# Rotary halves exchanged by SBUF transfers instead of TensorE, with the sums one block later and weight chunks asked for later from another queue

## The chip, the cores and the metric

The kernel runs on one core of a Trainium2 chip. A core has five engines, each with an instruction queue of its own that runs strictly in order: TensorE (PE) for matmuls, VectorE (DVE), ScalarE (ACT), GpSimd (POOL) and SyncE (SP), which here only issues transfers (DMA). They wait for each other through semaphores. The metric is the device time of one execution, in microseconds (us). Lower is better.

## The reference

The reference runs two transformer blocks on a sequence of 256 tokens with 1024 features, in float32. What matters here is the first attention of the second block, a differential attention with 8 heads, each with two query and two key parts of 64 features. Queries and keys are rotated before they meet:

```python
def apply_rope(x, cos, sin):
    half = x.shape[-1] // 2
    x1, x2 = x[..., :half], x[..., half:]
    ...
    return jnp.concatenate([x1 * c - x2 * s, x2 * c + x1 * s], axis=-1)

def diff_attention(hn, w_qkv, w_o, lq1, lk1, lq2, lk2, subln_g, lambda_init, cos, sin):
    ...
    q = apply_rope(q.reshape(B, S, 2 * H, d), cos, sin).reshape(B, S, H, 2, d)
    k = apply_rope(k.reshape(B, S, 2 * H, d), cos, sin).reshape(B, S, H, 2, d)
    ...
        p = jax.nn.softmax(s, axis=-1)
        a = p[:, :, 0] - lam * p[:, :, 1]
        return jnp.einsum('bqhk,bkhe->bqhe', a, v)
    ...
    o = rms_norm(o, subln_g, SUBLN_EPS) * (1.0 - lambda_init)
    return o.reshape(B, S, DIFF_V_WIDTH) @ w_o
```

After it come the output projection, a squared-ReLU MLP, and a latent attention with an MLP of its own, which the change touches only through constants.

## The kernel before

All weights arrive as one stream of chunks of 1 MB, each of two units (128 partitions by 1024 floats). Five chunks fit in the buffer `raw` (`NR`). Each unit is split into a high part (`whi`, made by ACT) and a low part (`wlo`, made by DVE), which together hold the float32 value; five units fit there (`NS`). A product is three matmuls: high by high, high by low, low by high. A unit can be split once the unit five places back has been used.

`schedule()` writes one list of steps. Every engine's program walks through this same list and runs its part of each step, so the order of the list is the order on each queue. In the stage around the change, `for hh in range(8)` with g = 0 and g = 8 makes the query block and then the key block of each head: `block` is 24 matmuls in two halves of 12 with a call in between. After it stands `rope`: ACT copies the block out of PSUM into `sg`, and POOL multiplies that copy with the cosines into `hm`. Half a block later stands `rope_end`: PE multiplies the copy with the constant matrix `rot`, which exchanges the halves and puts the sign on, into the other half of the same PSUM bank; DVE multiplies that with the sines (line 2545) and adds the cosine part (two adds of 64 partitions for a query, line 2550; one for a key, line 2552). After the block, `feed()` appends a `split` of the unit that has found room, and after each second one a `load` of a chunk, which SP issues once DVE's low part of the freed units is done.

The work of the attention heads is laid between blocks by `side.nudge()`, which is called twice per block (once between its halves, once behind it) and advances at most two parts. Head `hh` starts when the rotations of its query and key were emitted at least `rest[0]` nudges ago. Its steps are `diff_masks` and `diff` (PE: 2 + 8 matmuls), `softmax` (DVE: four maxima, line 2514; ACT: four exponentials, line 2221), `diff_mix` (DVE: a reciprocal at line 2572 up to two large operations at line 2581). Four nudges later comes `p_turn` (PE transposes, line 1939) and `p_copy` (ACT), then `times_v` (PE), `diff_square` (ACT, line 2262), `rstd` (DVE line 2310, POOL line 2619), `diff_scaled` (DVE line 2280), and `diff_turn` (PE, line 1978) with the copies of `part` (ACT and DVE). Heads 6 and 7 start during the output projection that follows, in which each unit is four groups of three matmuls of 512 columns (`row` steps).

Seen from DVE, each head has a round: four maxima, a wait for ACT's exponentials, the mix, a low part, the sums of a key, the part of the head two before, `rstd` of the head before and a wait for POOL, `diff_scaled`, another low part, the sums of a query, and the next head's maxima.

The lines that say this best:

```python
    def rope_end(at, rope):
        t_q[at], born[at] = next(rope), side.now
        yield
    ...
            tk = block(b, 0, unit(("qk", g + hh)), n1, side.nudge)
            rope = roped(("kT", hh) if g else ("qT", hh), not g, b, tk, 1.0 if g else 0.125, by_r)
            next(rope)
            side.nudge()
            feed()
            side.soon(rope_end(g + hh, rope))
```

## Time and profile before

| what | value |
|---|---|
| median of 3 runs | 1132.99 us (1132.96 to 1134.18) |
| the profiled execution's own time | 1132.69 us |
| its span, first to last instruction | 1131.4 us |
| PE busy | 1118.9 us, 99% of the span |
| DVE busy | 822.2 us, 73% |
| ACT busy | 638.4 us, 56% |
| POOL busy | 54.0 us, 5% |
| granted clock of PE | 1.000 over the whole span |
| stage of the 16 blocks | from about 574.4 to 643.6 us of the span |

The busy share of an engine is an average over stages, and PE's matmul ends are modelled, so 99% says that PE seldom stood empty and not how much room other engines have. The views used below give the start of an instruction and its duration. Where an engine stood idle before an instruction, the row has in brackets for how long and what released it. Instructions of one engine overlap a little in their records, so the distance between two starts, and not the recorded duration, is what an instruction costs its queue.

### The profile page before, as it was taken

Reading aid. Unit: us, or ns where it says so; the run is one execution under the profiler, and the core shown is the slowest. Engines: PE = TensorE matmul, PEld = TensorE weight load, DVE = VectorE, ACT = ScalarE, POOL = GpSimd, SP = SyncE. Lnnn points to the kernel's source line nnn. Section 1 sums busy time; section 2 is a strip of 40 time slices with the busy share of each in tenths; the row PEclk is TensorE's granted clock in tenths of the full one; section 3 lists DMA queues with packets and bytes.
Section 4 is the critical chain, followed back from the end, with each engine's and each line's share of the span. In section 5 each row is a group of like instructions: output and inputs, shape, how many; then the busy total and the mean of one; then the engine's idle time right before and its main releaser. Section 6 shows DMA issues by size and latency. Waiting matters only on the chain.

```text
span 1131.4 us, 16859 instructions
## 1 busy us (share of the span) xinstructions
PE 1118.9 (99%) x6545; PEld 980.3 (87%) x6545; DVE 822.2 (73%) x1417; ACT 638.4 (56%) x1205; POOL 54.0 (5%) x68
## 2 busy tenths in 40 slices
PE   9999999999999999999999999999999999999997
PEld 7998989799987888888899988888889988888886
DVE  6988878798666766666777777666667866766665
ACT  6664444856757754555755556444556654555553
POOL 2100000000001000000012300000001100000000
PEclk9999999999999999999999999999999999999999
DMA  9989989494232766666453326555554434655530
GB/s 385 421 318 390 368 319 352 138 336 162 94 113 75 250 209 224 214 224 207 145 187 112 118 107 224 190 185 189 189 181 168 164 112 152 209 191 190 191 129 37
DMA packets 33920, 231.10 MB, mean 204 GB/s; under 512 B 3729, under 2 KB 5169, under 8 KB 6450
## 3 DMA queue, kind: packets, MB, share of 16 engines
q1 hardware_dynamic: 31536, 225.59, 55.1%
q10 hardware_dynamic: 2306, 4.45, 1.2%
q8 instruction: 52, 0.85, 0.3%
q14 instruction: 26, 0.21, 0.0%
HBM read 228.95 MB, written 1.07 MB: 203 GB/s over the span
## 4 chain that ended last, share of the span: by engine, by line
PE 87%; DVE 6%; ACT 4%; issue 1%; DMA 1%; POOL 1%; ACTq 0%; DVEq 0%; POOLq 0%
PE ps L1727 43%; PE pacc L1727 43%; DVE wlo L2283 1%; ACT whi L2009 1%; ACT arena L2116 1%; DMA cl<-in_cols 1%; ACT wk L2221 1%; POOL st L2619 1%; DVE st L2514 0%; PE ps L1864 0%; DVE wk L2508 0%; DVE wlo L2293 0%; PE ps L1939 0%; DVE h L2405 0%; ACT arena L2009 0%
## 5 line engine op out<-in xcount | busy, mean ns | idle before, releaser
L2283 DVE TENSOR_TENSOR wlo<-raw,whi 128x1024 fp32r<-128x1024 f32 x346 | 415.0, 1223 | 115.3 <-ACT whi L2009 114.9
L1727 PE MATMUL ps<-both,whi 128*128 128x256 f32 (+2 forms) x1728 | 457.2, 339 | 1.2 <-DVE both L2380 0.6
L2009 ACT ACTIVATE whi<-raw 128x1024 fp32r<-128x1024 f32 x346 | 360.5, 1057 | 94.8 <-PE ps L1727 49.8
L1727 PE MATMUL ps<-both,wlo 128*128 128x256 f32 x1264 | 348.6, 281 | 0.0
L1727 PEld LDWEIGHTS ps<-both,whi 128*128 128x128 f32 (+1 forms) x1728 | 294.5, 189 | 41.8 <-issue 2.7
L1727 PEld LDWEIGHTS ps<-both,wlo 128*128 128x128 f32 x1264 | 236.2, 189 | 2.9
L1727 PE MATMUL pacc<-whi,both 128*128 128x512 f32 (+2 forms) x352 | 106.4, 383 | 1.0 <-ACT both L2132 0.6
L2009 ACT ACTIVATE sg<-ps 128x256 f32<-128x256 f32 (+1 forms) x98 | 37.3, 380 | 100.3 <-PE ps L1727 100.3
L1727 PE MATMUL pacc<-whi,mhi 128*128 128x512 f32 x228 | 90.7, 398 | 0.0
L1727 PE MATMUL pacc<-whi,mlo 128*128 128x512 f32 x228 | 89.5, 392 | 0.0
L2303 DVE SCALAR_TENSOR_TENSOR raw<-raw,silu_c 128x1024 f32<-128x1024 f32 x72 | 89.4, 1249 | 0.1
L1727 PE MATMUL pacc<-wlo,mhi 128*128 128x512 f32 x228 | 89.1, 391 | 0.0
L1727 PEld LDWEIGHTS pacc<-whi,both 128*128 128x128 f32 x352 | 64.0, 188 | 13.8 <-issue 1.3
L1727 PE MATMUL pacc<-both,whi 128*128 128x256 f32 x384 | 71.8, 293 | 0.1
L1727 PE MATMUL pacc<-whi,hhi 128*128 128x512 f32 x172 | 68.1, 396 | 0.0
L1727 PE MATMUL pacc<-whi,hlo 128*128 128x512 f32 x172 | 67.4, 392 | 0.0
L1727 PE MATMUL pacc<-wlo,hhi 128*128 128x512 f32 x172 | 67.2, 391 | 0.0
L2619 POOL TENSOR_TENSOR st<-st,mod 128x1 f32<-128x1 f32 (+1 forms) x34 | 20.3, 599 | 962.1 <-DVE st L2315 795.0
L1727 PE MATMUL pacc<-wlo,both 128*128 128x512 f32 (+2 forms) x176 | 62.9, 376 | 0.0
L1727 PEld LDWEIGHTS pacc<-both,whi 128*128 128x128 f32 x384 | 58.2, 190 | 1.1 <-issue 0.2
L2352 DVE TENSOR_TENSOR hm<-ps,sg 128x256 f32<-128x256 f32 x64 | 27.1, 423 | 44.1 <-ACT sg L2009 44.0
L1727 PEld LDWEIGHTS pacc<-whi,mlo 128*128 128x128 f32 x228 | 42.8, 188 | 10.3
(283 smaller groups left out, 1473.0 us busy)
## 6 DMA issues: line engine op xcount, KB each, us to landing
raw<-in_stream SPq DMA_DIRECT2D x213, 1024.0 KB, 5.0
gates<-gate_rows ACTq DMA_DIRECT2D x3, 512.0 KB, 5.6
h<-in_x SPq DMA_DIRECT2D x2, 512.0 KB, 4.2
cst<-in_const ACTq DMA_DIRECT2D x1, 1024.0 KB, 4.8
arena<-bias_rows ACTq DMA_DIRECT2D x1, 1024.0 KB, 22.5
arena<-in_final_g SPq DMA_DIRECT2D x1, 512.0 KB, 5.7
out<-tmp SPq DMA_DIRECT2D x2, 256.0 KB, 2.0
out<-tmp ACTq DMA_DIRECT2D x2, 256.0 KB, 2.3
```

Of the source, the lines that this page charges most:

```text
L1727: return e.matmul(o, a, b, start=start, stop=stop)
L2009: return e.activation(o, a, ACT.Copy, **how)
L2116: e.activation(m.arena[:, 6144 + 512 * st.n:6656 + 512 * st.n], m.h[:, st.i, half(st.f)], ACT.Square, scale=D ** -0.5, accum_out=m.stat(st ...
L2221: e.activation(m.wk[:, st.dst, a:a + n], src[:, a:a + n], ACT.Exp, bias=m.stat(st.mx + i), accum_out=m.stat(st.sm + i)).then_inc(S["exp"], 1)
L2283: return e.tensor_tensor(o, a, hi.bitcast(F32), ALU.subtract)
L2303: e.scalar_tensor_tensor(src, src, 1.0, m.silu_c[:, :], ALU.mult, ALU.mult, accum_out=m.adac[:, k:k + 1]).then_inc(S["ada"], 1)
L2352: e.tensor_tensor(u, m.bank(st.b)[:, 0:T], m.sg[:, st.m, :], ALU.add).then_inc(S["sums"], 1)
L2619: e.tensor_tensor(m.stat(r, width), m.stat(v, width), ex, ALU.pow).then_inc(S["xr"], 1)
```

## The change

For 15 of the 16 rotations (all but the last key), the step `rope_end` is replaced. `rope_swap`: ACT copies the block from PSUM into a place in the arena (three places in turn); POOL multiplies with the cosines as before; SP waits for the copy and issues four transfers from SBUF to SBUF, each of 32 partitions by 1 KB, that put each 32 partitions where their partner half lies. `rope_close`: DVE waits for the transfers, multiplies with the sines, and adds the cosine part. The sign now sits in the sine table, and the matrix `rot` is an unsigned exchange, also for the rotations that still use it. `rope_close` stands behind the next block's `rope_swap`, ahead of the heads' steps of that place, half a block later than `rope_end` did; `rest[0]` is 3 instead of 2 in this stage, counted from there. The PSUM bank is given back when the copy is done.

In this stage the weight chunks are issued by ACT's queue instead of SP's, and their step is written one and a half blocks later: `feed()` notes it as owed, the middle of the next block makes it due, and the middle of the one after issues it. What is left at the end of the stage is issued there by two calls, still on ACT. Then loads go back to SP.

```diff
@@ -242,13 +242,27 @@
             return [(P * k, P, COLS["kv_in_g"] + k) for k in range(8)]
         return []
 
+    owed, due, loader = [], [0], ["sp"]
+
     def load_chunk():
+        if loader[0] == "act":
+            owed.append(0)
+        else:
+            load_next()
+
+    def load_due():
+        for _ in range(due[0]):
+            load_next()
+        due[0] = len(owed)
+        owed.clear()
+
+    def load_next():
         n = pos["chunk"]
         if 2 * n >= len(stream):
             return
         pos["chunk"] += 1
         free = [t for u in (2 * (n - NR), 2 * (n - NR) + 1) for t in raw_free.get(u, [])]
-        add("load", chunk=n, free=latest(*free))
+        add("load", chunk=n, free=latest(*free), lane=loader[0])
 
     def feed(until=None, limit=100):
         while not hold and limit and pos["unit"] < (until or len(stream)):
@@ -1280,6 +1294,22 @@
         ys.give(yb, t)
         yield t
 
+    slots, swaps = Places([Place(n) for n in range(3)]), Counter()
+
+    def swapped(dst, split, b, tk, s, by):
+        slot = slots.take()
+        n, (at, t_tables) = slot.at, by
+        x, y = tick("rpc"), tick("rpz")
+        swaps[n] += 64
+        add("rope_swap", b=b.at, full=tk, s=s, n=n, free=slot.free, at=at, tables=t_tables, copied=x)
+        banks.give(b, x)
+        yield
+        sine = tick("rps")
+        add("rope_close", n=n, cosine=y, swapped=(f"swap{n}", swaps[n]), sine=sine, at=at, dst=dst, split=split)
+        t = tick("rpd", 2 if split else 1)
+        slots.give(slot, t)
+        yield t
+
     turns, by_r = [], []
 
     def during_v():
@@ -1353,17 +1383,34 @@
         t_q[at], born[at] = next(rope), side.now
         yield
 
+    pending, rest[0], loader[0] = [], 3, "act"
+
+    def halfway():
+        load_due()
+        side.nudge()
+
     for hh in range(8):
         for g in (0, 8):
             if hh == 7:
                 banks.retire(fix[2:4] if g else fix[0:2])
             b = banks.take()
-            tk = block(b, 0, unit(("qk", g + hh)), n1, side.nudge)
-            rope = roped(("kT", hh) if g else ("qT", hh), not g, b, tk, 1.0 if g else 0.125, by_r)
+            tk = block(b, 0, unit(("qk", g + hh)), n1, halfway)
+            last = g and hh == 7
+            rope = (roped if last else swapped)(("kT", hh) if g else ("qT", hh), not g, b, tk, 1.0 if g else 0.125, by_r)
             next(rope)
+            if pending:
+                at, was = pending.pop()
+                t_q[at], born[at] = next(was), side.now
             side.nudge()
             feed()
-            side.soon(rope_end(g + hh, rope))
+            if last:
+                side.soon(rope_end(g + hh, rope))
+            else:
+                pending.append((g + hh, rope))
+    load_due()
+    load_due()
+    loader[0] = "sp"
+    rest[0] = 2
     while banks.leaving:
         side.step(False)
     cross = Whole([(n1, ("cl", COLS["mlp_g"]), None, list)])
@@ -1548,7 +1595,7 @@
 
     "xsq", "xg", "xnew", "xrow", "xz", "xzd", "xah", "xhi", "xlo", "phi", "plo", "fin", "wa", "wb",
 
-    "ixc", "ixt", "mod", "g8", "masks", "tabc",
+    "rpc", "rpz", "swap0", "swap1", "swap2", "ixc", "ixt", "mod", "g8", "masks", "tabc",
 
     "lows", "sums", "sg", "hm", "hhi", "hlo", "rsilu", "rgate",
 
@@ -1630,6 +1677,10 @@
         self.ul = self.view(4096, 2, T)
         self.fg = self.arena[:, 6144:7168]
 
+    def swap_slot(self, n):
+        x, y = self.view(4096, 8, T), self.view(11776, 3, T)
+        return x[:, n, :], x[:, 3 + n, :], y[:, n, :]
+
     def view(self, at, n, width):
         return self.arena[:, at:at + n * width].rearrange("p (n r) -> p n r", n=n)
 
@@ -1701,10 +1752,16 @@
     e.dma_start(m.h[:, 0, :], d["x"][0:P, :]).then_inc(S["x0"], 16)
     e.dma_start(m.h[:, 1, :], d["x"][P:T, :]).then_inc(S["x1"], 16)
     for st in steps:
-        if st.kind == "load":
+        if st.kind == "load" and st.lane == "sp":
             q.room(st.free)
             n = st.chunk % NR
             e.dma_start(m.raw[:, n, :], d["stream"][st.chunk]).then_inc(S[f"raw{n}"], 16)
+        elif st.kind == "rope_swap":
+            q.wait_ge(*st.copied)
+            x, s, _ = m.swap_slot(st.n)
+            for a in range(0, P, 32):
+                c = a ^ 32
+                e.dma_start(s[a:a + 32, :], x[c:c + 32, :]).then_inc(S[f"swap{st.n}"], 16)
         elif st.kind == "lambda_load":
             q.wait_ge(*st.after)
             e.dma_start(m.lrow, bass.AP(tensor=d["lam"].tensor, offset=d["lam"].offset, ap=[[0, P], [1, 256]])).then_inc(S["lamrow"], 16)
@@ -2023,6 +2080,10 @@
                 t.then_inc(S["hi"], 1)
             else:
                 copy(hi, raw).then_inc(S["hi"], 1)
+        elif kind == "load" and st.lane == "act":
+            q.room(st.free)
+            n = st.chunk % NR
+            e.dma_start(m.raw[:, n, :], d["stream"][st.chunk]).then_inc(S[f"raw{n}"], 16)
         elif kind == "opening":
             for f in range(2):
                 q.wait_ge("acc", f + 1)
@@ -2248,6 +2309,10 @@
             q.wait_ge(*st.full)
             q.room(st.x_free)
             copy(m.sg[:, st.x, :], m.bank(st.b)[:, 0:T], scale=st.s).then_inc(S["rpx"], 1)
+        elif kind == "rope_swap":
+            q.wait_ge(*st.full)
+            q.room(st.free)
+            copy(m.swap_slot(st.n)[0], m.bank(st.b)[:, 0:T], scale=st.s).then_inc(S["rpc"], 1)
         elif kind == "lambda":
             q.wait_ge("lam", 2)
             e.activation(m.stat(st.le, 2), m.stat(st.ls, 2), ACT.Exp).then_inc(S["lexp"], 1)
@@ -2550,6 +2615,19 @@
                     e.tensor_tensor(to[r, 2 * n + c, :], x[r, :], y[r, :], ALU.add).then_inc(S["rpd"], 1)
             else:
                 e.tensor_tensor(o, o, y, ALU.add).then_inc(S["rpd"], 1)
+        elif kind == "rope_close":
+            what, h = st.dst
+            _, s, y = m.swap_slot(st.n)
+            q.wait_ge(*st.swapped)
+            q.wait_ge(*st.cosine)
+            o = s if st.split else m.kT[:, h, :]
+            e.tensor_tensor(o, s, m.rope_table(st.at, "sin"), ALU.mult).then_inc(S["rps"], 1)
+            q.wait_ge(*st.sine)
+            if st.split:
+                for c, r in enumerate(LOHI):
+                    e.tensor_tensor(m.qT[r, 2 * h + c, :], s[r, :], y[r, :], ALU.add).then_inc(S["rpd"], 1)
+            else:
+                e.tensor_tensor(o, o, y, ALU.add).then_inc(S["rpd"], 1)
         elif kind == "lambda":
             q.wait_ge("lamrow", 16)
             l4, lp = m.lrow.rearrange("p (a d) -> p a d", a=4), m.arena[:, 10496:10624].rearrange("p (a d) -> p a d", a=2)
@@ -2639,6 +2717,11 @@
             if st.tables:
                 q.wait_ge(*st.tables)
             e.tensor_tensor(m.hm[:, st.y, :], m.sg[:, st.x, :], m.rope_table(st.at, "cos"), ALU.mult).then_inc(S["rpy"], 1)
+        elif kind == "rope_swap":
+            q.wait_ge(*st.copied)
+            q.wait_ge(*st.tables)
+            x, _, y = m.swap_slot(st.n)
+            e.tensor_tensor(y, x, m.rope_table(st.at, "cos"), ALU.mult).then_inc(S["rpz"], 1)
 
 
 def build(nc, stream, x, c_row, cols, const, rel, lam, final_g, out):
@@ -2667,10 +2750,7 @@
     put("ident", np.eye(P))
     r = np.zeros((P, P))
     for m in range(P):
-        if m % 64 < 32:
-            r[m + 32, m] = -1.0
-        else:
-            r[m - 32, m] = 1.0
+        r[m + 32 if m % 64 < 32 else m - 32, m] = 1.0
     put("rot", r)
     put("flip", np.eye(P)[::-1])
     put("tri", (i[:, None] >= i[None, :]).astype(np.float32))
@@ -2680,7 +2760,7 @@
     inv = (np.float32(10000.0) ** (-np.arange(0, 64, 2, dtype=np.float32) / np.float32(64))).astype(np.float32)
     ang = (np.arange(T, dtype=np.float32)[:, None] * inv[None, :]).astype(np.float32)
     put("cos", np.cos(ang).astype(np.float32).T[i % 32])
-    put("sin", np.sin(ang).astype(np.float32).T[i % 32])
+    put("sin", np.sin(ang).astype(np.float32).T[i % 32] * np.where(i % 64 < 32, -1.0, 1.0)[:, None].astype(np.float32))
     t = np.arange(T)
     m = np.where(t[None, :] > t[:, None], MASKED, 0.0)
     put("topk", m.reshape(2, P, T).transpose(1, 0, 2).reshape(P, 2 * T))
```

## Rows read from the trace of the kernel before

**Rows 1.** Busy time of each engine over the whole span

```profile
PE 1118.9 (99%) x6545; PEld 980.3 (87%) x6545; DVE 822.2 (73%) x1417; ACT 638.4 (56%) x1205; POOL 54.0 (5%) x68
```

**Rows 2.** Timeline of PE around one rotation (start, duration, operation)

```profile
617.88 0.28 PE L1727 MATMUL ps<-both,wlo 128*128 128x256 f32 x1
...
618.24 0.28 PE L1727 MATMUL ps<-both,wlo 128*128 128x256 f32 x1
618.36 0.60 PE L1727 MATMUL pacc<-sg,cst 128*128 128x256 f32 x2
...
619.03 0.28 PE L1727 MATMUL ps<-both,wlo 128*128 128x256 f32 x1
```

**Rows 3.** Timeline of PE: the mask matmuls that begin heads 0 and 5

```profile
587.99 0.52 PE L1727 MATMUL pacc<-causalr,identr 128*128 128x384 f32 x2
...
634.10 0.60 PE L1727 MATMUL ps<-causalr,identr 128*128 128x384 f32 x2
```

**Rows 4.** Timeline of DVE: the maxima of heads 0, 1, 4 and 5

```profile
589.20 1.28 DVE L2514 TENSOR_REDUCE st<-pacc 128x1 f32<-128x128 f32 x4 [0.48 <-PE pacc L1727]
...
597.78 1.28 DVE L2514 TENSOR_REDUCE st<-ps 128x1 f32<-128x128 f32 x4 [0.57 <-PE ps L1727]
...
627.62 1.15 DVE L2514 TENSOR_REDUCE st<-ps 128x1 f32<-128x128 f32 x4
...
637.59 1.15 DVE L2514 TENSOR_REDUCE st<-ps 128x1 f32<-128x128 f32 x4
```

**Rows 5.** Timeline of DVE: between the maxima of heads 0 and 1, and 4 and 5

```profile
595.89 0.41 DVE L2545 TENSOR_TENSOR sg<-pacc,arena 128x256 f32<-128x256 f32 x1
...
630.03 0.17 DVE L2572 RECIPROCAL st<-st 128x2 f32<-128x2 f32 x1 [1.26 <-ACT wk L2221]
...
631.15 1.22 DVE L2283 TENSOR_TENSOR wlo<-raw,whi 128x1024 fp32r<-128x1024 f32 x1
632.29 0.42 DVE L2545 TENSOR_TENSOR arena<-ps,arena 128x256 f32<-128x256 f32 x1
632.74 0.51 DVE L2552 TENSOR_TENSOR arena<-arena,hm 128x256 f32<-128x256 f32 x1
...
634.52 0.61 DVE L2280 TENSOR_SCALAR wk<-pacc,st 128x128 f32<-128x128 f32 x2 [0.81 <-POOL st L2619]
...
636.25 0.41 DVE L2545 TENSOR_TENSOR sg<-pacc,arena 128x256 f32<-128x256 f32 x1
```

**Rows 6.** Timeline of DVE and PE: the end of head 7's mix and its transposes

```profile
655.99 1.14 DVE L2514 TENSOR_REDUCE st<-ps 128x1 f32<-128x128 f32 x4
...
658.85 0.75 DVE L2581 SCALAR_TENSOR_TENSOR wk<-wk,st 128x128 f32<-128x128 f32 x2
...
659.99 0.49 PE L1939 MATMUL ps<-cst,wk 128*128 128x128 f32 x3
```

**Rows 7.** ACT's copies of two query blocks, and ACT's copy of head 4's part

```profile
578.99 0.38 ACT L2009 ACTIVATE sg<-ps 128x256 f32<-128x256 f32 x1
...
630.82 0.39 ACT L2009 ACTIVATE sg<-pacc 128x256 f32<-128x256 f32 x1
...
647.29 0.47 ACT L2009 ACTIVATE n2hi<-ps,mod 128x256 fp32r<-128x256 f32 x1 [2.01 <-PE ps L1978]
```

**Rows 8.** Issues on SP, and DMA issues by line with size and us to landing

```profile
0.73 0.37 SPq L1701 DMA_DIRECT2D h<-in_x  x1
1.16 0.42 SPq L1702 DMA_DIRECT2D h<-in_x  x1
...
648.77 0.33 SPq L1707 DMA_DIRECT2D raw<-in_stream  x1
...
out<-tmp SPq DMA_DIRECT2D x2, 256.0 KB, 2.0
...
wk<-in_rel ACTq DMA_DIRECT2D x1, 1.0 KB, 4.6
```

**Rows 9.** DVE's adds of a query, all 24 (ns minimum, median, maximum)

```profile
L2550 DVE TENSOR_TENSOR arena<-sg,hm x24: 416/423/951, 581.9 to 916.8; 64x256 f32<-64x256 f32 x24
```

## The prediction

> **What bounds the kernel now.** I read the busy shares first, then the timeline of each engine through the stage of the 16 blocks and the projection behind it. The shares say that PE is the bound: 99% against 73% for DVE [rows 1]. In this stage PE does stand back to back. A change that takes matmuls away should then give their time back. The timelines of PE and DVE side by side say something else. PE begins the masks of head 0 at 587.99 and those of head 5 at 634.10, five heads in 46.11 us [rows 3]. DVE begins the maxima of the same heads at 589.20 and 637.59, 48.39 us [rows 4]. So DVE falls behind: its maxima start 1.2 us after the masks at head 0 and 3.5 us after them at head 5. Before the first two it waited for PE (0.48 and 0.57 us in brackets); before the later ones no bracket stands, because DVE's own queue was late. A round takes DVE 637.59 − 627.62 = 9.97 us [rows 4] and PE 46.11 / 5 = 9.2 on average. In a round DVE is idle only for 1.26 us, behind ACT's exponentials, and 0.81 us, behind POOL [rows 5]. Both waits hang on DVE's own earlier instructions, and a faster PE shortens neither.
>
> PE feels this only where it next needs DVE. The tightest place is the transposes of head 7: DVE's last mix operation ends at 658.85 + 0.75 = 659.60, and PE takes the result at 659.99 [rows 6]. Less than 0.4 us of room is left there. So from head 1's maxima to that point the path is DVE's queue, and PE is ahead of it by reserves that are used up by the end.
>
> **What is taken away.** Around a rotation the low-part matmuls start at 618.24 and 619.03, where neighbours are 0.36 us apart [rows 2]: a rotation costs PE 0.43 us. 15 of them are 15 × 0.43 = 6.5 us. On PE alone that would be the gain.
>
> **Where it goes.** A PE round becomes 9.2 − 2 × 0.43, some 8.4 us, against DVE's 9.97. Two results of DVE are then late. Mix to transposes: the mix ends 659.60 − 655.99 = 3.6 us after the maxima begin [rows 6]. A head's key: its sums end 632.74 + 0.51 − 627.62 = 5.6 us after the maxima of the head before [rows 4, 5]. PE needs that key 0.4 us after its masks, so masks can begin no sooner than 5.2 us behind the previous maxima. By my count this binds from head 3 on, and PE waits about 1 us per round: the removed matmuls turn into waits. The order of DVE's instructions is the same as before, since nothing of DVE stood between the old place of the sums and the new one. Their number is the same too: one multiplication and one or two adds. So a steady round stays at 9.97 us.
>
> **What the swap costs.** Let S be the time from ACT's copy to all four transfers landed. Two issues on SP began 0.43 us apart [rows 8], so the fourth begins 1.3 us after the first. No transfer between places of SBUF is in the trace. The nearest rows for landing are the 256 KB written at the end, 2.0 us, and, as the upper end, 1 KB asked for beside a load of constants, 4.6 us [rows 8]. With 0.1 us for the semaphore, S is 3.4 by the first and 6.0 by the second. A transfer of 32 KB has less to move than 256 KB, so I take 3.2. At its lower end S is 1.4 us plus almost nothing.
>
> In a steady round ACT begins the copy of a query 630.82 − 627.62 = 3.2 us after the maxima [rows 4, 7] and ends it at 3.6. DVE comes to that query's sums at 636.25 − 627.62 = 8.6 [rows 4, 5]. S may be up to 5.0 us, then, and is hidden. A key has more time still. Between heads 0 and 1 no earlier head's norm lies in the way and DVE comes at 595.89 − 589.20 = 6.7 [rows 4, 5]; with S = 3.2 the swap lands at 6.8. It costs 0.1.
>
> At the start: the first copy ends at 578.99 + 0.38 = 579.37 [rows 7], its swap lands at 582.6. Behind it DVE has in order the query's sums (0.45 + 0.88), a low part (632.29 − 631.15 = 1.14), the key's sums (0.9), a low part (1.14) and the next query's sums (1.33): 5.8 us in all by the distances of [rows 5] and the add of [rows 9] taken twice. Head 0's maxima come at 588.4 instead of 589.20. PE delivers head 0's products before that, being three rotations ahead. Head 1 follows after 597.78 − 0.57 − 589.20 = 8.0 us of DVE's own work and the 0.1: 596.5 instead of 597.78. DVE's queue is now 1.3 us earlier, because it no longer waits for PE there, and keeps that to head 5.
>
> **The loads on ACT.** Eight issues of about 0.33 us [rows 8] go to a queue that idles 44% [rows 1]. In a round their wait for DVE's low part is already met, as they stand behind ACT's next high part. The last is different. It waits for the low part whose end the old row shows, where SP issued at 648.77 [rows 8]. ACT's in-order queue now stands in that wait, and behind it are head 4's copy, which ACT had done from 647.29 [rows 7], and the squares of head 5, for which DVE waits. Copy, squares and issue take about 1.6 us after the low part; DVE has about 1.1 us of its own work there. I count 0.6 us of delay on DVE, an estimate between nothing and 1.6. Chunks still arrive in time: a chunk asked for five chunks ahead has about four rounds.
>
> The sum: DVE earlier by 1.3, later by 0.6, plus the room of 0.35 us at head 7's transposes (659.99 − 659.60, less a semaphore) gives 1.0 us. Behind that place everything hangs on PE as before. From the profiled execution's 1132.7: 1131.7; the median stands 0.3 above it, so **1132.0 us**, no change that can be measured. A kernel like this tells a difference from none at about 0.2%, 2.3 us.
>
> **A rule against the change.** POOL's cosine product runs beside DVE. The adds with two operands in SBUF took 416 ns at best and 951 at worst [rows 9]; the sine product, which read PSUM, 0.41 to 0.42 in all rows [rows 5]. The Trainium skill, GPSIMD Engine Reference, section 1 (Specifications), says that GpSimd shares its SBUF interfaces with VectorE and that they contend when a DVE instruction has two SBUF inputs. The sine product now has two, and the spread of the adds agrees with the rule. By the rule a contended product would cost up to the adds' 0.53 us more, in each of 15 rotations up to 8 us; by the steady key product, which lies beside POOL's work, nothing was seen yet. I give it a part of the slower case.
>
> The same skill, DMA: Bandwidth & Descriptors, section Anatomy of one DMA, gives a fixed cost of about 2.0 us per transfer. With it S is 3.4 and the gain 0.6 us instead of 1.0.
>
> **Rivals.**
> (1) PE is the bound after all: DVE's round shortens with PE's, for instance because its lag was harmless. Then 6.5 us come through: 1126.2. For it: PE without gaps, 99% [rows 1]. Against it: the lag that grows from head to head and the missing brackets [rows 3, 4]. 0.14; another 0.08 for half of it, 2.5 to 5 us, if DVE's rounds get a few tenths shorter.
> (2) The swap is late, and the sums hold DVE's queue with low parts and maxima behind them. It decides from S = 5.0 in steady rounds; earlier, at the start, each 0.1 us above 3.1 costs up to 0.2. With S = 5.5: 2.4 later at the first maxima, 2.4 at the next, 1 at the third, 0.5 in each of four rounds, 7.8 us in sum, less the 1.0: 1139.8. For it: the row of 4.6 us. Against it: in a round the query's swap is issued before the load, since ACT makes that copy ahead of it. 0.12, with the contention above in it.
> (3) My forecast, 0.66, with a range of its own of 1129.5 to 1134.8: S between 2.8 and 4.0, ACT's last wait between 0 and 1.6.
>
> The range of 8 in 10 is 1127.0 to 1136.5. It leaves out most of (1) and most of (2). Faster by over 0.2%: 0.14 + 0.07 and 0.03 of the forecast = 0.24. Slower: 0.13. Within: 0.63.
>
> **What would show it.** Right, if PE shows brackets before diff matmuls and transposes from head 3 on, in sum 5 us or more, if DVE's maxima stay 9.9 to 10.1 us apart from head 1 to 5 with no bracket before the sums, and if ACT stands before the last load. Wrong, if the maxima come 8.6 to 9.3 us apart (rival 1), or if brackets behind DMA stand before the sine products in steady rounds (rival 2). A PE that reads on without gaps while the time stays would break the whole chain.

## The result, and the profile after

The changed kernel takes 1151.21 us (median of 5 runs, 1150.71 to 1153.21), the kernel before 1133.01 us beside it. The ratio is 1.0165, 95% interval 1.0155 to 1.0176: slower by 18.2 us. I had forecast 1132.0 us and a range that ended at 1136.5, so the forecast is wrong. The profiled execution has a span of 1151.4 us. Its own time is 1153.12 us, one of the longer of the five, so the profiled spans of the two kernels lie 20.0 us apart and the medians 18.2.

The busy times of the engines, over the whole span:

```profile
PE 1121.6 (97%) x6515; PEld 978.8 (85%) x6515; DVE 825.5 (72%) x1417; ACT 637.0 (55%) x1205; POOL 55.0 (5%) x68
```

PE has 30 matmuls fewer than in [rows 1], as it should, and is busy for 97% instead of 99% of a longer span. DVE has as many instructions as before. So it is not work that was added; it is mostly waiting. PE's busy time is 2.7 us more although 6.5 us of matmuls are gone; its clock fell in four places, as the end of this text shows. The waits on DVE and on PE say for whom (total us, times, longest):

```profile
DVE arena L2624 <- DMA arena<-arena: 16.8, 8, 3.9
```

```profile
PE pacc L1784 <- DVE arena L2630: 7.1, 5, 1.7
PE ps L1996 <- DVE wk L2659: 4.1, 3, 2.6
PE ps L1784 <- DVE arena L2610: 2.5, 1, 2.5
```

L2624 is the sine product, which reads the exchanged copy: DVE stands before it for the transfers. PE stands for DVE's sums of a key (L2630), for its mix (L2659), and once for the last key (L2610). DVE's timeline shows the rhythm that comes of it, to be held against [rows 4, 5]:

```profile
592.50 0.43 DVE L2624 TENSOR_TENSOR arena<-arena 128x256 f32<-128x256 f32 x1 [3.87 <-DMA arena<-arena]
...
593.86 1.15 DVE L2579 TENSOR_REDUCE st<-pacc 128x1 f32<-128x128 f32 x4
...
604.64 0.43 DVE L2624 TENSOR_TENSOR arena<-arena 128x256 f32<-128x256 f32 x1 [3.04 <-DMA arena<-arena]
...
609.54 1.22 DVE L2348 TENSOR_TENSOR wlo<-raw,whi 128x1024 fp32r<-128x1024 f32 x1
610.68 0.95 DVE L2624 TENSOR_TENSOR arena<-arena 128x256 f32<-128x256 f32 x1
...
642.06 1.15 DVE L2579 TENSOR_REDUCE st<-pacc 128x1 f32<-128x128 f32 x4
```

Head 0's maxima start at 593.86 instead of 589.20, head 1's at 606.01 (in the next fence) instead of 597.78, head 4's at 642.06 instead of 627.62. The first steady rounds take 12.1 us each: (642.06 − 593.86) / 4 = 12.05. Before, it was 9.97 [rows 4]. Each round waits anew before a query's sine product (L2624). The key's product at 610.68 doesn't wait, but takes 0.95 us instead of 0.42 [rows 5].

The chain of waits shows a round as a closed loop (start, duration, what was waited for or worked on):

```profile
606.01 0.63 DVE st L2579 x2
...
607.38 1.00 ACT wk L2282 x5
608.38 0.95 ACT whi L2066
609.33 0.28 ACT arena L2066
609.63 0.51 SPq L1764
...
610.18 0.59 SPq L1764
...
610.82 0.59 SPq L1764
...
611.45 5.27 DMA arena<-arena
...
616.74 0.43 DVE arena L2624
```

Maxima, ACT's exponentials, the high part and the query's copy take 3.6 us, as in the forecast. Then SP issues four transfers, and the last one, issued from 611.45, lands 5.27 us later. It has landed at 616.72, and copy to last landing is 616.72 − 609.61 = **7.1 us**. The sums and the next maxima follow. The loop holds none of PE's work. The next three rounds of the same chain bear it out: from copy to last landing they take 6.9, 7.1 and 7.4 us, and the rounds 11.9, 12.1 and 12.4, each time 5.0 us more.

One more row says what else went out meanwhile. It is ACT's issue of a 1 MB weight chunk, in the same window, and behind it stand the DMA issues by line (KB each, median us to landing):

```profile
610.79 0.33 ACTq L2086 DMA_DIRECT2D raw<-in_stream  x1
```

```profile
arena<-arena SPq DMA_DIRECT2D x60, 32.0 KB, 3.6
...
raw<-in_stream ACTq DMA_DIRECT2D x8, 1024.0 KB, 5.5
```

The load goes out before the third and the fourth transfer (610.82 and 611.45). These two take 5.2 and 5.3 us to land, though they are a 32nd of its size; the two ahead of the load take 1.8 and 1.9. The load's own time of issue is no accident either. It waits until DVE's low part (L2348) has freed its buffer, and that low part ends at 609.54 + 1.22 = 610.76, 0.03 us before the load starts. Copy and low part both hang on the maxima, so the load falls at the same place of every round.

### The profile page after: what moved, and what is told of

Same layout as the page of the kernel before. It is cut to its first block, busy times and chain, and to the rows that moved or that the text cites. A ratio compares the mean times of both kernels' runs of the same rounds, so it can differ in the third digit from the quotient of the medians.

```text
span 1151.4 us, 16844 instructions
## 1 busy us (share of the span) xinstructions
PE 1121.6 (97%) x6515; PEld 978.8 (85%) x6515; DVE 825.5 (72%) x1417; ACT 637.0 (55%) x1205; POOL 55.0 (5%) x68
## 4 chain that ended last, share of the span: by engine, by line
PE 84%; DVE 5%; ACT 4%; DMA 4%; SPq 1%; issue 1%; POOL 1%; ACTq 0%; DVEq 0%; POOLq 0%
PE pacc L1784 42%; PE ps L1784 40%; DMA arena<-arena 3%; SPq L1764 1%; ACT wk L2282 1%; ACT whi L2066 1%; DVE wlo L2348 1%; ACT arena L2177 1%; DMA cl<-in_cols 1%; DVE st L2579 1%; POOL st L2697 1%; DVE arena L2628 0%; PE ps L1921 0%; DVE wlo L2358 0%; ACT arena L2066 0%
## 5 line engine op out<-in xcount | busy, mean ns | idle before, releaser
L2348 DVE TENSOR_TENSOR wlo<-raw,whi 128x1024 fp32r<-128x1024 f32 x346 | 415.5, 1225 | 114.3 <-ACT whi L2066 114.0
L1784 PE MATMUL ps<-both,whi 128*128 128x256 f32 (+1 forms) x1712 | 452.7, 339 | 1.7 <-DVE both L2445 0.6
L1784 PEld LDWEIGHTS ps<-both,whi 128*128 128x128 f32 x1712 | 291.7, 190 | 42.2 <-issue 3.0
L2066 ACT ACTIVATE sg<-ps 128x256 f32<-128x256 f32 (+1 forms) x88 | 33.5, 380 | 90.3 <-PE ps L1784 90.3
L1784 PEld LDWEIGHTS pacc<-both,whi 128*128 128x128 f32 x400 | 60.7, 191 | 1.0 <-issue 0.3
```

The lines of the kernel that those rows point to most:

```text
L1784: return e.matmul(o, a, b, start=start, stop=stop)
L2066: return e.activation(o, a, ACT.Copy, **how)
L2348: return e.tensor_tensor(o, a, hi.bitcast(F32), ALU.subtract)
```

## The experiments

Eleven kernels part five suspects: the transfers' latency, the loads on ACT, the moved sums, POOL beside DVE, and PE. Times are medians; the ratio is to the kernel before, timed beside each (1132.7 to 1133.0 us), with its 95% interval.

**No transfers.** The four transfers are left out and the sine product reads the copy itself, so the exchange of halves is left out.

```
-            e.dma_start(s[a:a + 32, :], x[c:c + 32, :]).then_inc(S[f"swap{st.n}"], 16)
...
-            q.wait_ge(*st.swapped)
...
-            e.tensor_tensor(o, s, m.rope_table(st.at, "sin"), ALU.mult).then_inc(S["rps"], 1)
+            e.tensor_tensor(o, x, m.rope_table(st.at, "sin"), ALU.mult).then_inc(S["rps"], 1)
```

> The changed kernel without the four transfers of a swap: the sums read the unexchanged copy, so the exchange of the halves is left out of 15 rotations; everything else, the order and the loads on ACT too, is as changed. Theory A (the changed kernel's round of 12.1 us is a loop through the transfers): the loop is gone, DVE's own queue sets the round, 10.0 to 10.5 us (10.5 if the key's sine product stays at 0.95 us instead of 0.42 beside POOL), and the time is 1131 to 1136 us. Theory B (the moved sums and the loads on ACT cost most): 1145 us or more. Theory C (once nothing is waited for, PE is the bound): rounds of 8.4 us and 1126 us.

Measured: 1134.86 us, ratio 1.0017 (1.0007 to 1.0026). The transfers cost 16 us of the 18. But without them, and without PE's 30 rotation matmuls, the kernel is still not faster than before: the 6.5 us of PE don't come through.

**PE's rotation in the new order.** The sums stay ahead of the heads' steps and the loads stay late and on ACT; the rotation is PE's again.

```
-            rope = (roped if last else swapped)(("kT", hh) if g else ("qT", hh), not g, b, tk, 1.0 if g else 0.125, by_r)
+            rope = roped(("kT", hh) if g else ("qT", hh), not g, b, tk, 1.0 if g else 0.125, by_r)
```

> The changed kernel with all rotations made by TensorE again, but with the sums where the change puts them (behind the next block, three nudges ahead of the head) and the loads on ACT one and a half blocks later. Theory A: the time of the kernel before within 1.5 us, 1132 to 1135 us, since only the transfers cost. Theory B: 1140 us or more.

Measured: 1132.61 us, ratio 0.9998 (0.9989 to 1.0007). The moved sums and the loads on ACT cost nothing by themselves. Whatever harm the loads do, they do it together with the transfers.

**The load at the end of the block.** `load_due()` moves from the middle of the block to behind its copy.

```
     def halfway():
-        load_due()
         side.nudge()
...
             next(rope)
+            load_due()
```

> The changed kernel with each load issued by ACT behind the next copy instead of in the middle of a block, so that a chunk of 1 MB no longer starts while the query's four swap transfers are being issued. Theory A1 (the last swap transfer takes 5.3 us only because it shares the DMA engines with the load): it lands in about 2 us, the loop shrinks from 12.1 to at most 10 us, and the time falls to 1132 to 1138 us. Theory A2 (a transfer from SBUF to SBUF is slow by itself, and the four issues of 0.63 us in a row are most of it): 1146 us or more.

Measured: 1153.19 us, ratio 1.0179 (1.0162 to 1.0196). This told nothing apart. The loads went out at the same times (598.62, 610.96, 622.95) as in the changed kernel (598.65, 610.79, 622.88). In both kernels a load goes out within 0.04 us of the end of DVE's low part that frees its buffer, so the move of one place in ACT's list changed nothing; the expectation had left that wait out. An edit of the list must be read in the trace before it counts as an experiment.

**One transfer of 128 partitions** in place of the four of 32; the exchange is left out, the copy is carried over as it is.

```
-            for a in range(0, P, 32):
-                c = a ^ 32
-                e.dma_start(s[a:a + 32, :], x[c:c + 32, :]).then_inc(S[f"swap{st.n}"], 16)
+            e.dma_start(s, x).then_inc(S[f"swap{st.n}"], 16)
...
```

> The changed kernel with one transfer of 128 partitions in place of four of 32: the same bytes, but a straight copy, so the exchange of the halves is left out. The loads stay where the change has them. Issue time falls by 3 x 0.63 = 1.9 us per rotation, and the query's transfer is issued ahead of the load. Theory A1: it lands in about 2 us, S is under 3.5 us, and the time is 1131 to 1137 us. If only the number of issues counted and not the load: the round falls by 1.9 us from 12.1 to 10.2, which gives 1137 to 1141 us. Theory B: no change, 1149 us or more.

Measured: 1135.48 us, ratio 1.0024 (1.0014 to 1.0033). The DMA issues by line show that as much data now lands in 2.0 us:

```profile
arena<-arena SPq DMA_DIRECT2D x15, 128.0 KB, 2.0
```

That is the median. The loads still go out on ACT, but 1.1 us behind the query's only transfer, which lands in 1.9 to 2.0 us. The key's transfer starts 0.9 us behind the load (614.52 after 613.58) and takes 4.5 us; no round waits for it, since a key has more time. So a transfer through SBUF isn't slow by nature. What is left open here is whether the number of issues or the order against the load did it. The next two answer that.

**The loads back on SP,** at their late places, behind the four transfers in the same queue.

```
-        add("load", chunk=n, free=latest(*free), lane=loader[0])
+        add("load", chunk=n, free=latest(*free), lane="sp")
```

> The changed kernel with the same loads at the same places of the list, but issued by SP's queue, the one that issues the swap transfers, instead of ACT's. The load then stands behind the query's four transfers in one queue. Theory A1 (the fourth transfer lands late because the load, issued from the other queue while SP is still issuing, is served with or ahead of it): the query's transfers land about 4.5 us after the copy, the sums are no longer waited for in steady rounds, rounds go from 12.1 to about 10.4 us, time 1134 to 1138 us. Theory A2 (transfers from SBUF to SBUF take 5 us whenever four are in a row): rounds stay near 12 us, 1148 us or more.

Measured: 1135.76 us, ratio 1.0030 (1.0019 to 1.0042). All four transfers are still there. They land in a median of 1.9 us, and DVE waits for them once, for 1.6 us at the start of the stage (583.09), and in no round:

```profile
arena<-arena SPq DMA_DIRECT2D x60, 32.0 KB, 1.9
```

The median hides half of the story. These are SP's issues of one round, first a query's four transfers, then the load, then a key's four, and below them the time to landing of the first four and of the last four:

```profile
622.76 2.41 SPq L1764 DMA_DIRECT2D arena<-arena  x4
625.21 0.58 SPq L1758 DMA_DIRECT2D raw<-in_stream  x1
625.83 2.41 SPq L1764 DMA_DIRECT2D arena<-arena  x4
```

```profile
DMA to landing us min/median/max: 1.8/1.9/2.2
...
DMA to landing us min/median/max: 3.9/4.2/4.7
```

The key's four, issued right behind the load, are as late as in the changed kernel, though now all stand in one queue. So a second queue isn't what makes a transfer late; standing behind the load is. It costs nothing here because the key's sums come late enough.

**The load ahead of the next split on ACT,** and so before the query's copy and its exchange.

```
     def halfway():
-        load_due()
         side.nudge()
...
             side.nudge()
+            load_due()
             feed()
```

> The changed kernel with each load on ACT's queue between the head's exponentials and the next high part, some 2.5 us earlier in the round than now. The load starts before the query's swap is issued instead of in its middle, and should land at about 7.5 us after the maxima instead of at 10.3. Theory A1: the last swap transfer lands with or shortly after the load, at 7.5 to 8.5, so rounds shrink from 12.1 to 10.4 or less, 1134 to 1140 us. Theory A2: no change, 1148 us or more.

Measured: 1138.41 us, ratio 1.0053 (1.0038 to 1.0068). The load now goes out while the exponentials run (600.30), 2.4 us before the first issue of the exchange (602.73); in the changed kernel it went out 1.2 us after that issue. The median landing is 2.0 us and the rounds are 10.35 us. The first transfer of a query, 2.4 us behind the load, takes 2.5 us and lands with it. ACT's queue, the number of issues and the bytes are those of the changed kernel; only the moment of the load against the transfers differs. At the end of the stage the two calls that issue what is left bring the old case back once: a load goes out at 644.97, 0.02 us before the third transfer of a query, the last two take 4.9 and 4.8 us, and DVE waits 1.22 us at 650.51. That is part of the 2.7 us between this run and the one before; the rest wasn't traced.

These two together show the cause: a small transfer that is issued while a 1 MB load is on its way lands about when that load does, in one queue as in two, and the loads take 4.9 to 5.8 us in the changed kernel. What counts is how late in the load's way the transfers start, and whether somebody waits for them. Which part of the way they share can't be read from these rows.

**Without transfers and without POOL's cosine product** (cut to one column; DVE's adds take the copy in its place), so exchange and cosine are left out.

```
...
-            e.tensor_tensor(y, x, m.rope_table(st.at, "cos"), ALU.mult).then_inc(S["rpz"], 1)
+            e.tensor_tensor(y[:, 0:1], x[:, 0:1], m.rope_table(st.at, "cos")[:, 0:1], ALU.mult).then_inc(S["rpz"], 1)
```

> The kernel without transfers (the exchange left out) in which POOL's cosine products are cut to one column and DVE adds the copy itself, so the cosine is left out too. DVE's instructions keep their number and size. If POOL's product beside it is what stretches the key's sine product from 0.42 to 0.95 us, it goes back to 0.42, rounds go from 10.36 to 9.8 or 9.9 us and the time to 1131 to 1133 us. If the two SBUF operands alone stretch it: rounds stay at 10.3 to 10.4 us and the time at 1134 to 1136.

Measured: 1129.61 us, ratio 0.9972 (0.9963 to 0.9982), 5.2 us less than without transfers alone. DVE's timeline, first of the run with the loads on SP (its rounds equal those without transfers), then of this one:

```profile
619.14 1.15 DVE L2579 TENSOR_REDUCE st<-pacc 128x1 f32<-128x128 f32 x4
623.81 0.95 DVE L2624 TENSOR_TENSOR arena<-arena 128x256 f32<-128x256 f32 x1
...
629.49 1.15 DVE L2579 TENSOR_REDUCE st<-pacc 128x1 f32<-128x128 f32 x4
```

```profile
614.69 1.15 DVE L2573 TENSOR_REDUCE st<-pacc 128x1 f32<-128x128 f32 x4
619.36 0.42 DVE L2617 TENSOR_TENSOR arena<-arena 128x256 f32<-128x256 f32 x1
...
624.51 1.15 DVE L2573 TENSOR_REDUCE st<-pacc 128x1 f32<-128x128 f32 x4
```

With POOL's product beside it, the key's sine product takes 0.95 us and the round 629.49 − 619.14 = 10.35. Without it, 0.42 and 624.51 − 614.69 = 9.82. Against the 9.97 before, 0.38 us in each of some five or six rounds is most of the 2 to 3 us that the kernels still lose whose transfers land in time. It is what the Trainium skill states in GPSIMD Engine Reference, section 1 (Specifications): the two engines contend when a DVE instruction reads both operands from SBUF. PE's rotation left that operand in PSUM; the transfer moved it to SBUF.

**Without DVE's part of the rotation.** No transfers, and POOL writes its product straight to the query or key. Sines, exchange and adds are left out.

```
-        sine = tick("rps")
+        sine = None
...
-            e.tensor_tensor(y, x, m.rope_table(st.at, "cos"), ALU.mult).then_inc(S["rpz"], 1)
+            e.tensor_tensor(o, x, cos, ALU.mult).then_inc(S["rpz"], 1)
```

> The kernel without transfers in which DVE does nothing for 15 rotations: POOL's cosine product goes straight into the place of the query or key; sines, exchange and adds are left out. DVE's round loses 2.7 to 2.9 us. Theory A (DVE's queue is what keeps the removed TensorE work from showing): PE becomes the bound at last, rounds 8.4 to 8.7 us, time 1126 to 1128 us. Theory D (something else, such as ACT's chain or the projection behind the stage, holds the time even with a free DVE): 1131 us or more.

Measured: 1125.97 us, ratio 0.9939 (0.9922 to 0.9956), 6.9 us less than before. DVE's timeline:

```profile
612.26 1.28 DVE L2572 TENSOR_REDUCE st<-pacc 128x1 f32<-128x128 f32 x4 [0.68 <-PE pacc L1777]
...
620.88 1.28 DVE L2572 TENSOR_REDUCE st<-pacc 128x1 f32<-128x128 f32 x4 [0.71 <-PE pacc L1777]
```

The brackets behind PE are back and the round is 8.62 us: PE is the bound, and its 6.5 us come through. So the gain was real and DVE's queue hid it.

**A version to beat both.** The loads are on SP, the exchange by four transfers stays, and POOL makes the query's two adds in place of DVE (the added lines stand in POOL's program). It computes all of the reference.

```
-            q.wait_ge(*st.sine)
-            if st.split:
-                for c, r in enumerate(LOHI):
-                    e.tensor_tensor(m.qT[r, 2 * h + c, :], s[r, :], y[r, :], ALU.add).then_inc(S["rpd"], 1)
...
+        elif kind == "rope_close" and st.split:
+            _, s, y = m.swap_slot(st.n)
+            q.wait_ge(*st.sine)
+            for c, r in enumerate(LOHI):
+                e.tensor_tensor(m.qT[r, 2 * st.dst[1] + c, :], s[r, :], y[r, :], ALU.add).then_inc(S["rpq"], 1)
+                q.wait_ge("rpq", 2 * st.nq + c + 1)
```

> The loads are issued by SP as in the run with the load on SP (1135.8 us), and the query's two adds are made by POOL in place of DVE; of a query's close DVE keeps the sine product alone. Theory (DVE's queue sets the rounds, 10.36 us in that run, and a PE round is 8.4 to 8.6): the round loses the two adds, about 0.87 us, so it becomes about 9.5 us, 0.5 us under the kernel before in five rounds, and the whole 1130.5 to 1132.5 us. Rival (POOL and DVE contend for SBUF, so what DVE no longer does comes back in slower products and maxima, or POOL's power, queued behind the adds, comes later and DVE waits for it): the round stays at 10.0 to 10.4 and the whole at 1134 to 1136 us.

Measured: **1129.65 us**, ratio 0.9977 (0.9968 to 0.9985): 3.1 us faster than before and 21.6 faster than the changed kernel. DVE's timeline of one round:

```profile
616.67 1.14 DVE L2579 TENSOR_REDUCE st<-pacc 128x1 f32<-128x128 f32 x4
...
621.33 0.97 DVE L2624 TENSOR_TENSOR arena<-arena 128x256 f32<-128x256 f32 x1
...
623.07 0.15 DVE L2375 SCALAR_TENSOR_TENSOR st<-st 128x2 f32<-128x2 f32 x1
624.02 0.61 DVE L2345 TENSOR_SCALAR wk<-ps,st 128x128 f32<-128x128 f32 x2 [0.80 <-POOL st L2694]
...
626.03 1.14 DVE L2579 TENSOR_REDUCE st<-pacc 128x1 f32<-128x128 f32 x4
```

The round is 9.36 us, a little under the 9.5 expected, and the whole is 0.9 us under the range of 1130.5 to 1132.5. POOL takes 1.54 us for the two adds, where DVE took 2 × 0.42 [rows 9], but DVE's wait for POOL stays at 0.80 (0.81 in [rows 5]), and none of its brackets in a round got longer.

**The key's add on POOL too.**

```
-            if not st.split:
-                q.wait_ge(*st.sine)
-                e.tensor_tensor(o, o, y, ALU.add).then_inc(S["rpd"], 1)
...
```

> As the run before, with the key's add on POOL as well. Theory: the round loses another 0.45 us, about 9.05 us, and PE's 8.6 us comes near; 1128.5 to 1131 us. Rival: the key comes later by POOL's slower add (1.1 to 1.2 us instead of 0.45), PE's masks, which need it, start later, and POOL's power behind it is late for DVE's mix; then no better than the run before, 1131.5 to 1136 us.

Measured: 1130.75 us, ratio 0.9985 (0.9977 to 0.9994). The time lies in the theory's range of 1128.5 to 1131, but the theory's round of 9.05 us did not come, and the whole is no better than the run before, as the rival has it. Its DVE timeline shows where the add's 0.43 us went:

```profile
619.26 1.14 DVE L2579 TENSOR_REDUCE st<-pacc 128x1 f32<-128x128 f32 x4
...
625.21 0.51 DVE L2375 SCALAR_TENSOR_TENSOR st<-st 128x2 f32<-128x2 f32 x1
626.59 0.61 DVE L2345 TENSOR_SCALAR wk<-ps,st 128x128 f32<-128x128 f32 x2 [0.88 <-POOL st L2691]
...
628.59 1.14 DVE L2579 TENSOR_REDUCE st<-pacc 128x1 f32<-128x128 f32 x4
```

The round is 9.33 us. The small operation on statistics, now beside POOL's add, takes 0.51 instead of 0.15, and the wait for POOL's power is 0.08 longer: 0.44 came back. The medians of the two runs differ by 1.1 us, but their single times overlap (1128.5 to 1133.0 and 1130.0 to 1133.5), so a difference between them isn't clear of the noise. The profiled execution of this kernel had a mean granted clock of 0.95, so its PE rows don't help.

**The kernel before with only the query's adds on POOL,** moved from DVE's program as above.

```
-        t = tick("rpd", 2 if split else 1)
+        t = tick("rpq", 2) if dst[0] == "qT" else tick("rpd", 2 if split else 1)
...
```

> The kernel before, PE's rotation and all, with the query's two adds on POOL and nothing else changed. Theory (both engines have to give up work: DVE's rounds of 9.97 us would fall to about 9.1, but PE with its rotations takes 9.2 to 9.5 a round and binds next): little, 1131.5 to 1132.7 us, well behind the 1129.7 us of the run that has the exchange by transfers and the adds on POOL; then the transfers are worth their 6.5 us of PE only where DVE's queue is relieved too. Rival (the whole gain of that run is the adds on POOL, and taking the rotation from PE gave nothing): 1129.3 to 1130.3 us.

Measured: 1132.89 us, ratio 0.9999 (0.9990 to 1.0008). DVE's timeline:

```profile
616.20 1.28 DVE L2514 TENSOR_REDUCE st<-ps 128x1 f32<-128x128 f32 x4 [0.47 <-PE ps L1727]
...
625.66 1.28 DVE L2514 TENSOR_REDUCE st<-ps 128x1 f32<-128x128 f32 x4 [0.49 <-PE ps L1727]
```

DVE is relieved, and at once stands behind PE: the round is 9.46 us, that of a PE with its two rotations. Neither half of the pair gains anything alone (the transfers alone, with their loads on SP, take 1135.8 us); together they give 3.1 us.

## Why the prediction was wrong

**What bounds the kernel: right.** DVE's queue set the stage, with PE's reserves shrinking behind it. Taking 6.5 us from PE gave nothing while DVE kept its rounds (no transfers: 1134.9), and gave 6.9 us when DVE's part was gone (1126.0). Rival 1 is excluded. The forecast's 9.2 us for a PE round was a mean over five heads; a steady one takes 9.46 by the last run, half a microsecond under DVE's.

**The place of the danger: right, its size wrong.** The step that failed is S in "What the swap costs", the time from ACT's copy to the four transfers landed. I put it at 3.2 us; it was 7.1 in the steady rounds and 8.3 before head 0's maxima, where SP was still issuing the transfers of the key ahead. Two of its terms were too small. The issues stand 0.63 us apart on SP, and I had taken 0.43 from two issues of another kind [rows 8]: 1.8 us to the start of the fourth instead of 1.3. And the landing is 5.27 us instead of 1.8. Even my upper bound of 6.0, built on the 4.6 us of [rows 8], was passed. The other steps of that sum held: copy at 3.6, and against the old round a loss from S = 5.0 on. With S = 7.1 the same rule gives a round of 9.97 + 7.1 − 5.0 = 12.1 us, as measured. The 2.0 us that the forecast takes from the Trainium skill, DMA: Bandwidth & Descriptors, stand in that section for transfers issued by way of GpSimd; SP's, with nothing ahead of them, landed in 1.8 to 1.9 us.

**Why the landing was late.** I argued that the query's swap is issued before the load. That looked at where each stands in its program and not at the 2.5 us that SP needs for four issues. I also wrote that in a round the loads' wait for DVE's low part is already met. It is not: every load of the stage in the changed kernel goes out within 0.04 us of the end of that low part, in a round 1.2 us after ACT's copy, and this puts it between the second and the third issue. In the runs with the load on SP, with the load elsewhere on ACT and with one transfer, the rounds' query transfers don't stand just behind a load, and land in 1.8 to 2.6 us. My part on the loads looked only at what queues behind them on ACT; what their data does to small transfers issued behind them was not priced at all.

**Rival 2 was the mechanism,** with S = 5.5 and 7.8 us as its price, and 0.12 as its chance. Its slope was right (round = S + 5.0, three rounds above). Its threshold of 5.0 was never tried on its own: with the slower key product DVE comes to the query's sums at 9.0 us, and without any waiting the round is already 10.35. Late landings add 4.7 us to head 0's maxima (589.20 to 593.86), 3.6 at the next and 2.1 in each of four rounds, 16.8 us at head 5's maxima (637.59 to 654.41). The next round adds 1.6, and PE's products for head 6 start 18.4 us late (667.91 instead of 649.49). The last 1.6 us are TensorE's clock. PE had stood for 2.5 us, and from 667.63 on the chain of waits runs over PE alone (seen up to 690 us):

```profile
667.63 0.45 PE L1784 MATMUL ps<-causalr,identr 128*128 128x384 f32 x1 [2.51 <-DVE arena L2610]
667.91 2.30 PE L1784 MATMUL ps<-arena 128*128 128x128 f32 x8
...
672.23 0.52 PE L1784 MATMUL ps<-causalr,identr 128*128 128x384 f32 x2
```

In the kernel before, the same matmuls:

```profile
649.49 1.47 PE L1727 MATMUL ps<-arena 128*128 128x128 f32 x8
...
652.19 0.51 PE L1727 MATMUL ps<-causalr,identr 128*128 128x384 f32 x2
```

From the products of head 6 to the masks of head 7 it is 4.32 us instead of 2.70, and the masks are 20.0 us late, which is all of the difference between the two spans. A range that ends before a threshold whose crossing costs a round 1 us for each 1 us is too narrow when the only bound for S lies beyond it.

**The rule on POOL and DVE: right, and it deserved more.** I gave it a part of one case because the old key's product showed no sign of it. But that product read PSUM, so its row could not show it. It cost 0.53 us on every steady key. Taking POOL's product away whole gave 5.2 us over the stage; how much of that is this contention, and how much what else went away with the product, the run doesn't part. The contention turns "the same" into the 1.002 to 1.003 of the runs whose transfers land in time.

**The loads on ACT in themselves and the moved sums: right,** nothing (1132.6). The 0.6 us of the last load's wait didn't show in the whole.

## What to carry to other kernels

Work taken from an engine that looks full is worth nothing until the queue that sets the rounds is found; here PE's round (9.46) and DVE's (9.97) are 0.5 us apart, and only a pair of edits, one for each, made the kernel faster. When an edit puts a DMA on a round's path, price it with the issues in sequence and with every large load that is on its way in that time, ask what releases that load, and issue it behind the small transfers that somebody soon waits for; in the same queue that order is fixed. A median over all transfers doesn't tell whether the awaited ones are the quick ones. When a result moves from PSUM to SBUF, ask which engine now meets its reader at SBUF.

## What the runs showed of the hardware

A transfer of 32 KB between places of SBUF lands mostly in 1.8 to 1.9 us when no load is on its way. Issued behind a 1 MB load that is, it lands about when the load does: 5.2 us right behind it, 3.9 to 4.7 us in the 2.5 us after that in the same queue, 2.5 us when it starts 2.4 us behind a load with nothing between them. The issues stand some 0.6 us apart on SP.

POOL pays for the contention as well: in the fastest kernel that computes all, its cosine product of the query takes 1.6 us beside DVE's low part and key product, and that of the key 0.7 us (POOL's timeline at 620.40 and 623.96).

TensorE's clock fell in four places where PE had stood waiting. This is PE's timeline of the changed kernel, and below it the stretches of 1 us around it (length, busy and count of PE, PEld, DVE, ACT and POOL, granted clock, DMA share, GB/s):

```profile
597.53 0.55 PE L1996 MATMUL ps<-cst,wk 128*128 128x128 f32 x3 [2.59 <-DVE wk L2659]
...
600.08 2.86 PE L1784 MATMUL ps<-arena 128*128 128x128 f32 x8 [1.65 <-DVE arena L2630]
```

```profile
600.00:601.00 1.00, 0.92 (x3) 0.89 (x4) 1.00 (x1) 0.00 (x0) 0.52 (x1) 0.57 0.55 172
...
604.00:605.00 1.00, 1.00 (x10) 1.00 (x10) 0.36 (x1) 0.00 (x0) 0.00 (x0) 1.00 0.01 3
...
669.00:670.00 1.00, 1.00 (x5) 0.83 (x4) 0.35 (x2) 0.59 (x1) 0.61 (x1) 0.50 0.93 377
```

PE waited 2.59 and then 1.65 us, was granted 0.50, which is 1.2 GHz, up to about 603.5, and was back at 2.4 GHz by 604. Its eight matmuls took 2.86 us instead of the 1.55 of the same eight at 636.20. The same came at 624.33 (after waits of 1.38 and 1.66 us) and at 648.29 (1.36 and 1.67), but not at 612.23 and 636.20, which had one wait each, of 1.65 and 1.51. It fell after a single wait of 2.51 us at 667.63 too, and was at 0.50 from about 668.4 to 671.8. In the three rounds the fall cost nothing, since their loop holds nothing of PE. Behind the last wait PE is the path, and there it cost the 1.6 us shown above, on top of the wait.
